# Gathering the expert rows as turned halves from row 48 on instead of from row 176 on

## The reference, cut to what matters

```
top_s, pos = lax.top_k(cand_s, PEER_TOPK)                 # 16 of 256 candidates, per token and head
experts = jnp.take_along_axis(cand_i, pos, axis=-1)
gates = jax.nn.softmax(top_s, axis=-1)
...
ub = u_tab[eb]
h = jax.nn.gelu(jnp.einsum('td,thed->the', xb, ub), approximate=False)
vb = v_tab[eb]
return jnp.einsum('the,thed->td', gb * h, vb)
```

## Time and profile before

| what | value |
|---|---|
| median of three runs | 1637.08 us |
| profiled execution | 1635.16 us |
| its span in the trace | 1633.4 us |
| PE busy | 1535.5 us (94%) |
| DVE busy | 1330.8 us (81%) |
| POOL busy | 566.1 us (35%) |

### The profile page before, as it was taken

One profiled execution on the slowest core, in us unless ns is written; L12 is line 12 of the kernel. 1 busy time (PEld: TensorE's weight loads), 2 busy tenths in 40 slices (PEclk: granted clock), 3 DMA queues, 4 the chain that ended last, 5 costly groups with the idle time before them and its releaser, 6 DMA issues.

```text
span 1633.4 us, 19189 instructions
## 1 busy us (share of the span) xinstructions
PE 1535.5 (94%) x6332; PEld 994.1 (61%) x6332; DVE 1330.8 (81%) x2279; ACT 603.4 (37%) x1554; POOL 566.1 (35%) x371
## 2 busy tenths in 40 slices
PE   9999999999999989888999898899998999999996
PEld 8999899988766556454555554455555344444442
DVE  5689999766877788988999998889988866666686
ACT  5433345634322223222332222456554422222242
POOL 0000110100112333433333232345336767756572
PEclk9999999999999999998999999999999999999998
DMA  6565553484799999999999999999999999999996
GB/s 253 187 243 186 183 172 139 157 331 157 298 426 428 426 427 421 416 394 394 408 415 408 405 390 392 408 399 406 394 384 389 383 408 418 419 415 417 409 340 244
DMA packets 69906, 567.17 MB, mean 347 GB/s; under 512 B 16847, under 2 KB 17519, under 8 KB 20591
## 3 DMA queue, kind: packets, MB, share of 16 engines
q0 software_dynamic: 50560, 445.59, 66.9%
q1 hardware_dynamic: 18580, 120.22, 19.6%
q10 hardware_dynamic: 672, 0.21, 0.1%
HBM read 665.68 MB, written 4.19 MB: 410 GB/s over the span
## 4 chain that ended last, share of the span: by engine, by line
PE 42%; DMA 33%; DVE 13%; issue 8%; ACT 2%; POOL 1%; POOLq 0%; DVEq 0%; SPq 0%; ACTq 0%
DMA uv_row<-in_uv_tab,eid 26%; PE psum L853 12%; PE psum L546 7%; PE psum L547 7%; PE psum L548 7%; DMA uv_row<-in_uv_tab,turned 5%; PE psum L946 4%; DVE scratch L1747 4%; DVE y_last L1760 1%; POOL uv_row L489 1%; PE psum L874 1%; PE psum L792 1%; DMA uv_row<-in_uv_tab,last_id 1%; ACT first_key L1259 1%; DMA w_raw<-in_w_stream 1%
## 5 line engine op out<-in xcount | busy, mean ns | idle before, releaser
L853 PE MATMUL psum<-uv_row,scratch 128*128 128x512 f32 x1560 | 737.0, 611 | 78.4 <-ACT scratch L1228 70.5
L1747 DVE CUSTOM_DVE_ANT_0 scratch<-uv_row,x 128x2048 bf16<-128x2048 f32 x250 | 572.5, 2290 | 161.0 <-DMA uv_row<-in_uv_tab,eid 78.4
L853 PEld LDWEIGHTS psum<-uv_row,scratch 128*128 128x128 f32 x1560 | 291.7, 193 | 416.0 <-issue 302.6
L489 POOL DMA_INDIRECT uv_row<-in_uv_tab,eid x176 | 282.6, 1606 | 539.2 <-DVE y_last L1760 329.8
L1206 ACT ACTIVATE dots<-dots 128x1 f32<-128x1 f32 x256 | 51.8, 202 | 644.5 <-DVE dots L1747 644.2
L489 POOL DMA_INDIRECT uv_row<-in_uv_tab,turned x156 | 243.2, 1559 | 108.5 <-PE psum L853 46.7
L546 PE MATMUL psum<-xT_hi,w_hi 128*128 128x256 f32 x640 | 183.7, 287 | 2.3 <-DVE w_lo L1339 2.1
L547 PE MATMUL psum<-xT_lo,w_hi 128*128 128x256 f32 x640 | 181.7, 284 | 0.0
L548 PE MATMUL psum<-xT_hi,w_lo 128*128 128x256 f32 x640 | 181.7, 284 | 0.0
L1339 DVE TENSOR_TENSOR w_lo<-w_raw,w_hi 128x2048 fp32r<-128x2048 f32 x62 | 141.7, 2287 | 28.7 <-ACT w_hi L1005 27.9
L1005 ACT ACTIVATE w_hi<-w_raw 128x2048 fp32r<-128x2048 f32 x62 | 118.8, 1915 | 85.8 <-DMA w_raw<-in_w_stream 85.8
(11 more groups left out here) (271 smaller groups left out, 1635.1 us busy)
## 6 DMA issues: line engine op xcount, KB each, us to landing
w_raw<-in_w_stream SPq DMA_DIRECT2D x63, 1024.0 KB, 4.8
dense_unit<-in_dense_u SPq DMA_DIRECT2D x16, 1024.0 KB, 11.3
dense_unit<-in_uv_tab SPq DMA_DIRECT2D x16, 1024.0 KB
wq_first<-in_w_stream SPq DMA_DIRECT2D x8, 1024.0 KB, 11.5
wq_third<-in_w_stream SPq DMA_DIRECT2D x4, 1024.0 KB, 11.9
uv_row<-in_uv_tab,eid POOLq DMA_INDIRECT x176, 20.9
uv_row<-in_uv_tab,turned POOLq DMA_INDIRECT x156, 23.4
xT_raw<-in_xT SPq DMA_DIRECT2D x4, 512.0 KB, 6.0
```

The costliest lines, as they stand in the source:

```text
L489: pool.indirect_dma_start(dst, None, tab, bass.IndirectOffsetOnAxis(ap=ids, axis=0), bounds_check=tab.shape[0] - 1, oob_is_err=False).then ...
L853: last = pe.matmul(bank(i, n), diag[k], row[k][:, D + n * 512:D + (n + 1) * 512], start=False, stop=True, skip_group_check=True)
L1747: dve.tensor_tensor_reduce(row[k][:, 0:D] if s < PLACES else product, row[k][:, 0:D], x1[:, ROW_OF[s][0], :], 1.0, 0.0, ALU.mult, ALU.add, ...
```

## The change

`SPLIT` becomes 48: heads 0, 1 and 2 of tile 0 are still gathered whole, and all rows from 48 to 253 as halves. `turn_last` follows to row 48 and `turn_tables` to row 40. The ids of halves are made head by head in `mark`: `eid` itself becomes the table of U ids (doubled in place), `v_id` is written from it crosswise. The turned weights are kept in a ring of 48 columns, for which ACT has two more waits on rows 47 earlier.

```diff
-SPLIT = VALUES_AT
+WHOLE_HEADS = [(0, 0), (0, 1), (0, 2)]
+SPLIT = len(WHOLE_HEADS) * TOP
-SPLITS = SLOTS - FIRST_SPLIT[0] + SLOTS - FIRST_SPLIT[1]
-TURN_AT = 123
+SPLITS = TI * SLOTS - SPLIT
+HELD = 48
+TURN_AT = 40
...
-                if s == SPLIT:
-                    pool.wait_ge(turn_ready, 1)
                 if split(s):
-                    c = split_col(s)
                     pool.wait_ge(dots_done, BEFORE_IT[s] + 1)
-                    gather(row[k][:, 0:D], halves, u_id[:, c:c + 1], u_in[k])
+                    gather(row[k][:, 0:D], halves, eid[:, i * SLOTS + j:i * SLOTS + j + 1], u_in[k])
                     if s > SPLIT:
                         v_half(s - 1)
...
                     act.wait_ge(weight_whole, s - SPLIT + 1)
-                    c = split_col(s)
+                    if s >= SPLIT + HELD:
+                        act.wait_ge(y_last_done, min(s - HELD + 1, JOIN_AT))
+                        act.wait_ge(diag_done, s - HELD + 1)
+                    c = s % HELD
...
-                dve.scalar_tensor_tensor(out=eid[:, q * TOP:(q + 1) * TOP], in0=of_dense[:, :], scalar=float(SKIP),
-                                         in1=posf[0][:, :], op0=ALU.mult, op1=ALU.add).then_inc(picked, 1)
+                ids = eid[:, q * TOP:(q + 1) * TOP]
+                last = dve.scalar_tensor_tensor(out=ids, in0=of_dense[:, :], scalar=float(SKIP), in1=posf[0][:, :],
+                                                op0=ALU.mult, op1=ALU.add)
+                if (i, h) not in WHOLE_HEADS:
+                    link(last)
+                    cols = slice(SPLIT_COL[i] + h * TOP, SPLIT_COL[i] + (h + 1) * TOP)
+                    dve.tensor_scalar(v_id[HALF:P, cols], ids[0:HALF], 2.0, 1.0, ALU.mult, ALU.add)
+                    link(dve.tensor_scalar(v_id[0:HALF, cols], ids[HALF:P], 2.0, 1.0, ALU.mult, ALU.add))
+                    last = dve.tensor_scalar(ids, ids, 2.0, None, ALU.mult)
+                last.then_inc(picked, 1)
...
             def turn_tables():
 
                 dve.tensor_copy(ident_turned[:, 0:HALF], ident[:, HALF:P])
-                dve.tensor_copy(ident_turned[:, HALF:P], ident[:, 0:HALF])
-                for i in range(TI):
-                    ids = eid[:, i * SLOTS + FIRST_SPLIT[i]:(i + 1) * SLOTS]
-                    cols = slice(SPLIT_COL[i], SPLIT_COL[i] + SLOTS - FIRST_SPLIT[i])
-                    dve.tensor_scalar(u_id[:, cols], ids, 2.0, None, ALU.mult)
-                    dve.tensor_scalar(v_id[HALF:P, cols], ids[0:HALF], 2.0, 1.0, ALU.mult, ALU.add)
-                    last = dve.tensor_scalar(v_id[0:HALF, cols], ids[HALF:P], 2.0, 1.0, ALU.mult, ALU.add)
+                last = dve.tensor_copy(ident_turned[:, HALF:P], ident[:, 0:HALF])
                 last.then_inc(turn_ready, 1)
...
                 if s == TURN_AT:
-                    dve.wait_ge(picked, TI * PH)
                     turn_tables()
```

More of the change, by code:

```diff
@@ L101 @@
 HALF = P // 2
-SPLIT = VALUES_AT
+WHOLE_HEADS = [(0, 0), (0, 1), (0, 2)]
+SPLIT = len(WHOLE_HEADS) * TOP
 SPLIT_USES = [sum(SPLIT <= r and PLACE[r] == PLACE[s] for r in range(s + 1)) for s in range(ALL)]
-FIRST_SPLIT = [min((ROW_OF[s][1] for s in range(SPLIT, ALL - TAIL) if ROW_OF[s][0] == i)) for i in range(TI)]
-SPLIT_COL = [0, SLOTS - FIRST_SPLIT[0]]
-SPLITS = SLOTS - FIRST_SPLIT[0] + SLOTS - FIRST_SPLIT[1]
-TURN_AT = 123
+SPLIT_COL = [-SPLIT, SLOTS - SPLIT]
+SPLITS = TI * SLOTS - SPLIT
+HELD = 48
+TURN_AT = 40
 def layer(nc, xT, x_tok, w_stream, w_kw, w_sub, conv_p, cln, bucket1h, rel_bias,
@@ L251, in layer @@
         dots = sb("dots", [P, TI * SLOTS])
-        turned = sb("turned", [P, 3 * SPLITS])
-        weight_turned = turned[:, 0:SPLITS]
-        u_id, v_id = (turned[:, n * SPLITS:(n + 1) * SPLITS].bitcast(I32) for n in (1, 2))
+        v_id = sb("v_id", [P, SPLITS], I32)
+        weight_turned = sb("weight_turned", [P, HELD])
         weight = sb("weight", [P, TI * SLOTS])
@@ L293, in split_col @@
             i, j = ROW_OF[s]
-            return SPLIT_COL[i] + j - FIRST_SPLIT[i]
+            return SPLIT_COL[i] + j
         turned_rows = nc.dram_tensor("turned_rows", (NH, P, S), F32, kind="Internal").ap()
@@ L1758, in add_last @@
                     dve.wait_ge(v_half_in[k], v_half_from[k] + 16 * SPLIT_USES[s])
-                    w = weight_turned[:, split_col(s):split_col(s) + 1]
+                    w = weight_turned[:, s % HELD:s % HELD + 1]
                 dve.scalar_tensor_tensor(out=y_last[:, i, :], in0=row[k][:, D + 3 * 512:2 * D], scalar=w,
```

## The result

The changed kernel takes 1639.27 us (median of 19 runs, 1631.58 to 1644.05), the kernel before, measured beside it 19 times, 1634.49 us. The ratio is 1.0021, with an interval of [1.0011, 1.0031]: slower by 3.4 us (the two medians lie 4.8 us apart). I had forecast 12.8 us less. The profiled execution has a span of 1638.7 us.

The account below looks back on a forecast made before the run. The prediction took the middle stage to be held by DMA, fed by buffers that come free late, and the late stage by PE. Terms -13.8 + 0.7 + 0.3 = -12.8 us gave 1624 us against 1637.08; range 1608 to 1646.

Parts of the forecast that it names:

- the one on POOL: Middle stage: twice as many gathers cost nothing, a pair taking 4.12 us against 4.34 us for each row.
- POOL becomes the bound: Rival, 680:1245: a pair of gathers takes 4.52 us or more, the stage 19 us more, 1656; chance 0.11.
- The late stage is held by PE, and nothing that the change does there shortens it: Late stage, 1280:1560: PE busy 98%; the prediction is wrong if this stage changes by more than 3 us.
- The gain: Middle stage, 680:1245: halves move 409 GB/s instead of 399, 551.2 us instead of 565, 13.8 us less.
- the early U half: Middle stage: a U half waits only for the dot and is issued about one row earlier; inside the 13.8 us.
- The turn: Halves: V into the partition 64 away may even out the engines; already in the late stage's rate, so 0.
- uneven engines: Rival, middle stage: the turn evens nothing, halves move 390 GB/s, 13.6 us more, 1651; chance 0.06.
- ACT and DVE: Middle stage: ACT's added activations put at 0, 6 us at worst; DVE's added work at 0.7 and 0.3 us.
- What the new profile was to show: Rows 48 to 176: length near 557 us, 405 to 417 GB/s, POOL some 75% busy, DVE 92%, longer U landings.
- The sign that I had named for POOL binding: Rows 48 to 176: gathers follow without a wait and DVE waits for landings at under 405 GB/s.

Follow-up runs that it names:

- e2: The kernel before with one more indirect DMA, moving nothing, for each of rows 128 to 175: 1647.95 us, ratio 1.008.
- e5: The changed kernel with rows 128 to 175 gathered whole and V landing in its own partition: 1645.7 us, ratio 1.0061 to the kernel before.
- e6: The changed kernel with rows 128 to 175 whole and the U half waiting for PE and add_last too: 1637.54 us, ratio 1.0014 to the kernel before.
- e4: The changed kernel with the dots of rows 128 to 175 over half of the columns: 1617.67 us, ratio 0.989 to the kernel before.
- e8: The changed kernel with rows 140 to 175 gathered whole again: 1624.94 us, ratio 0.9932 to the kernel before.
- e12: The kernel of e8 run once more, on another run's chip: 1621.95 us, ratio 0.993 to the kernel before.
- e3: The kernel before with the dots of rows 128 to 175 over half of the columns: 1633.96 us, ratio 0.9993.

## Why the prediction was wrong, point by point

**The step that failed is the one on POOL.** I took 2.06 us for a gather from the burst at 1245.49 and held 4.12 us for a pair against 4.34 us for a row. Both sides were taken from the wrong stretch. The row time of 4.45 us is the mean of 4.58 (380 us, 83 rows) before 1060 and 4.20 after, so POOL had to be held against 4.2 there. And in the burst 7 of 13 gathers started in a dot (2.45 us in the mean) and one in L1792, the chunk's comparison (L1794 in the changed kernel), whereas in 1060:1245 of the changed kernel 44 of 82 started in a dot (2.62 us) and 15 in the comparison (1.70 us): 2.26 us each with the gap, 4.51 us a pair, more than the 4.20 that a row had. The stage cut at 1060, as in the windows above, would have shown the 4.20. And I never asked which operations hold a gather up, only whether the dot does. In place of "it costs nothing", e2 shows 13 us for 48 gathers without a byte.

**The rival had the mechanism, the size of a pair by luck, and not the place.** "POOL becomes the bound" gave 4.52 us for a pair by its rows; measured is 4.51. That the two agree so closely is luck: the rival added gathers of 1.60 us in the mean and gaps of 0.66 us, the trace has about 1.96 us busy for each (160.32/82) and gaps of 0.30. It priced the stage as a whole at 19 us and had a chance of 0.11. It holds for 48 of 128 rows only; 205.2 - 200.3 = 4.9 us show there, and the rest shows later.

**"The late stage is held by PE, and nothing that the change does there shortens it"** was the second wrong step. DMA's share was 1.01 at 416 GB/s in the same rows from which I read PE's 98%, and between the dots of rows 176 and 254 the time follows the bytes: 137.2 MB in 343.2 us before, 140.0 in 350.9 in e2, 142.1 in 354.8 in the changed kernel, all at 399 to 401 GB/s, while PE's busy share falls from 98% to 96%. A stage in which DMA is full can't take over what an earlier one did not move. It cost 11.6 us, the largest single term, and I had allowed 3.

**The gain was right in size where POOL isn't short, and only in part in its reason.** 409 GB/s were predicted for the whole stage and 409 measured in 680:1060, where however 401 and not 399 was the start. 13.8 us x 80/127 rows = 8.7 us were expected for rows 48 to 128, less 1 for DVE; measured 6.9. I had given the gain to the early U half; by e5 and e6 the turn has the larger part of it (9 GB/s, against 5). With POOL's shortage taken away otherwise, e4 gives 415 GB/s in the last third. That e8 and e12 come out at 1624.9 and 1622.0 us, where the forecast of 1624 had been, is chance: they gather 36 of the 128 rows whole.

**The turn.** "Nothing is added" was right for the sum, since the rate of the late stage held it; e5 shows how much hung on it, 18.5 us over both stages. My rival "uneven engines" gave 13.6 us for the middle stage without its effect; e5 lost 374.1 - 367.1 = 7.0 us against whole rows in 80 of 127 rows, where that price makes 8.6; but its rate was 400 GB/s, not the rival's 390, so the agreement of the times is no proof of it. No row names an engine; that the unevenness is one of engines stays an inference. The Trainium skill, page "DMA: Bandwidth & Descriptors", section "The descriptor swizzle", has partitions 0 to 63 served by eight engines and 64 to 127 by the other eight; by that rule the turn spreads a token's two halves over two engines. No run here shows it.

**ACT and DVE** were put at 0 and 1 us. e4 has all of ACT's added work and is 16 us faster than its partner without it, which bears out the first. Less DVE time was worth nothing in the kernel before (e3); no run measures DVE's 1 us in the changed one.

**What the new profile was to show.** POOL some 75% busy or more in the stage: 443.28 of 565, 78%, with its waits for `add_last` down from 237.2 to 35.8 us ("below 60"). DVE 518.49 of 565, just under 92%. U landings longer: median 24.7 us instead of 22.0 up to 1060, but 9.2 instead of 20.8 behind it, the clearest sign of all that the issue binds. The stage by the gathers of rows 48 and 176: 1254.79 - 670.63 = 584.2 us instead of 570.2, while by the dots of these rows it is 565.4 instead of 567.4; the difference of the two views is the queue that has run dry. The sign that I had named for POOL binding, gathers without a wait and DVE waiting for landings at under 405 GB/s, is what 1060:1245 shows.

## What to carry to other kernels

When a change gives an in-order issuing engine more instructions, compare the issue time with the work's pace in the fastest stretch of the stage, not with its mean, and count what each issue is held up by: here an instruction of 0.99 us cost 2.0. Transfers that land sooner (9 us instead of 21) while the rate falls meant here that too few were asked for; where DMA is full later on, every byte not moved is paid there, so look for a loss behind the stage that caused it. A change that helps in one stage and hurts in another can be made in the one alone: going back to whole rows from 140 to 175 turned +0.2% into -0.7%.

## What the runs showed of the hardware that I had not expected

- An indirect DMA whose ids are all out of bounds costs GpSimd as much as a full one: 1.86 us in the mean beside 1.92 (e2, 1060:1245).
- Not only the dot holds up an indirect DMA on GpSimd. A DVE operation with one input and a scalar over 2048 columns (1.25 us) and a scalar_tensor_tensor with two inputs (2.28 us) do as well; the gather ends 0.85 to 0.88 us behind any of them. The searches do not: all 23 gathers that started in a MAX8 in 680:1060 of the changed kernel took 0.99 us and ended as little as 0.59 us behind it. Nor did every dot: 2 of the 215 gathers that started in a dot of the changed kernel, 0.02 and 0.04 us behind its start, took 0.99 us and were done before it.
- Gathering 8 KB halves without the turn brought no more GB/s than gathering 16 KB rows (400 against 401 in 680:1060), with it more (409): the partition to which the second half goes was worth more here than anything that halving gained. Why it matters, no row shows.
